# VectorE's order in the down product: the four additions to X ahead of the split of the moving operand

## The reference

```python
x = x + jnp.concatenate([ret, att], axis=-1) @ w_o[i]          # mixing, done before this stage
h = rmsnorm(x, ffn_norm_g[i])
x = x + (jax.nn.silu(h @ w_ffn_gate[i]) * (h @ w_ffn_up[i])) @ w_ffn_down[i]
gate = jax.nn.sigmoid(rmsnorm(x, ple_norm_g[i]) @ w_ple_gate[i])
x = x + gate * (p[i] @ w_ple_proj[i])
return rmsnorm(x, final_norm_g)
```

## Time and profile before

| what | value |
|---|---|
| time, median of 3 runs | 1270.57 us (1270.55 to 1271.13) |
| profiled execution, its own time | 1272.39 us |
| its span, first to last instruction | 1270.6 us |
| mean granted TensorE clock | 0.995 of full |
| TensorE (PE) busy | 1241.5 us, 98% |
| VectorE (DVE) busy | 732.4 us, 58% |
| ScalarE (ACT) busy | 480.2 us, 38% |
| GpSimd (POOL) busy | 492.5 us, 39% |

### The profile page before, as it was taken

How to read it: one execution, slowest core, us unless ns; L and a number is a source line. 1 busy time by engine, 2 the same in 40 slices (tenths; PEclk the granted TensorE clock), 3 DMA queues, 4 the chain that set the end, 5 groups by cost and what they waited for, 6 DMA issues and landing times.

```text
span 1270.6 us, 16751 instructions
## 1 busy us (share of the span) xinstructions
PE 1241.5 (98%) x6008; PEld 1043.8 (82%) x6008; DVE 732.4 (58%) x1194; ACT 480.2 (38%) x875; POOL 492.5 (39%) x510
## 2 busy tenths in 40 slices
PE   9899999989999999999999999999999999999997
PEld 8788888878888888888888888888888878788886
DVE  4554444477665326865444545444489999964433
ACT  6522222246665214533333333333354343414422
POOL 2343334441000002464334554434399887610011
PEclk9899999999999999999999999999999999999999
DMA  9411111010021500223323423323554554330002
GB/s 343 139 50 34 50 34 34 1 42 1 0 66 68 149 1 1 73 89 121 118 77 97 125 87 121 117 80 94 182 181 162 171 182 166 116 116 1 1 34 100
DMA packets 101933, 115.10 MB, mean 91 GB/s; under 512 B 4833, under 2 KB 67681, under 8 KB 101857
## 3 DMA queue, kind: packets, MB, share of 16 engines
q1 hardware_dynamic: 101424, 113.57, 27.5%
q10 hardware_dynamic: 432, 0.54, 0.1%
HBM read 90.49 MB, written 23.59 MB: 90 GB/s over the span
## 4 chain that ended last, share of the span: by engine, by line
PE 74%; issue 11%; POOL 6%; DVE 5%; DMA 2%; ACT 1%; SPq 0%; POOLq 0%; DVEq 0%; ACTq 0%
PE PS L1671 11%; PE PS L1672 10%; PE PS L1670 10%; PE PS L2004 4%; PE PS L2005 4%; PE PS L2006 4%; PE PS L206 3%; PE PS L208 3%; PE PS L207 3%; PE PS L997 3%; PE PS L1013 3%; PE PS L2356 2%; PE PS L2358 2%; PE PS L2357 2%; PE PS L791 2%
## 5 line engine op out<-in xcount | busy, mean ns | idle before, releaser
L206 PE MATMUL PS<-WF,HTH 128*128 128x512 f32 (+1 forms) x448 | 177.8, 397 | 6.8 <-DVE X L488 4.2
L208 PE MATMUL PS<-WF,HTL 128*128 128x512 f32 (+1 forms) x448 | 174.3, 389 | 0.0
L207 PE MATMUL PS<-WF,HTH 128*128 128x512 f32 (+1 forms) x448 | 174.1, 389 | 0.0
L1391 DVE TENSOR_TENSOR X<-X,PS 128x512 f32<-128x512 f32 x172 | 109.8, 677 | 51.6 <-PE PS L208 36.5
L1670 PE MATMUL PS<-HTH,WF 128*128 128x512 f32 x336 | 130.7, 389 | 0.0
L1671 PE MATMUL PS<-HTL,WF 128*128 128x512 f32 x336 | 130.7, 389 | 0.0
L1672 PE MATMUL PS<-HTH,WF 128*128 128x512 f32 x336 | 130.7, 389 | 0.0
L1603 DVE TENSOR_TENSOR WF<-RAW,WF 128x512 fp32r<-128x512 f32 x63 | 69.9, 1111 | 77.6 <-ACT WF L1593 77.6
L206 PEld LDWEIGHTS PS<-WF,HTH 128*128 128x128 f32 x448 | 85.0, 190 | 23.5 <-issue 4.9
L208 PEld LDWEIGHTS PS<-WF,HTL 128*128 128x128 f32 x448 | 84.8, 189 | 16.4
L1670 PE MATMUL PS<-WF 128*128 128x512 f32 x252 | 98.0, 389 | 0.0
(11 more groups left out here) (254 smaller groups left out, 2855.2 us busy)
## 6 DMA issues: line engine op xcount, KB each, us to landing
hid<-TMP SPq DMA_DIRECT2D x74, 256.0 KB, 2.3
TMP<-hid SPq DMA_DIRECT2D x25, 512.0 KB, 4.7
RAW<-in_w_ffn_gate SPq DMA_DIRECT2D x22, 512.0 KB, 4.1
RAW<-in_w_ffn_up SPq DMA_DIRECT2D x22, 512.0 KB, 5.4
RAW<-in_w_ffn_down SPq DMA_DIRECT2D x22, 512.0 KB, 4.1
X<-in_x SPq DMA_DIRECT2D x16, 512.0 KB, 6.0
RAW<-in_w_in SPq DMA_DIRECT2D x32, 256.0 KB, 3.6
TAB<-hid SPq DMA_DIRECT2D x9, 512.0 KB, 4.7
```

What stands on the lines that cost most here:

```text
L206: nc.tensor.matmul(dst, HTH[:, k, tok], w_h, start=(k == 0), stop=False)
L207: nc.tensor.matmul(dst, HTH[:, k, tok], w_l, start=False, stop=False)
L208: last = nc.tensor.matmul(dst, HTL[:, k, tok], w_h, start=False, stop=(k == K - 1))
L1391: nc.vector.tensor_tensor(x, x, src, ALU.add).then_inc(done, 1)
```

## The change

In the loop over the steps, the four additions come first, and the split (`ring_lo` or `down_lo`) behind them. The pieces and the two extra `down_lo` of step 33 keep their places behind both.

```diff
@@ -2087,12 +2087,12 @@
             for s in range(STEPS):
                 add_step(e, s, 0)
                 add_step(e, s, 1)
+                add_step(e, s, 2)
+                add_step(e, s, 3)
                 if s + 3 < STEPS:
                     ring_lo(e, s + 3)
                 elif s < STEPS - 1:
                     down_lo(e, LAST_ORDER[s + 3 - STEPS])
-                add_step(e, s, 2)
-                add_step(e, s, 3)
                 if s >= 18 and s % 4 == 2 and s <= 30:
                     piece_lo(e, (s - 10) // 4)
                 if s == STEPS - 2:
```

## The result

The changed kernel takes 1277.35 us (median of 6 runs, 1276.11 to 1278.16); beside it the kernel before took 1270.74 (6 runs). The ratio is 1.0050 with a 95% interval of 1.0038 to 1.0063: 6.6 us slower, forecast 4.2. The profiled execution took 1276.11 us, its span is 1274.3.

The account below looks back on a forecast made before the run. The prediction took TensorE to bound the stage, with VectorE close behind and its additions causing the stalls. Terms -0.4 + 1.6 + 0.8 + 2.2 = +4.2 us on 1270.57 gave 1274.8 us, range 1270.8 to 1277.4.

Parts of the forecast that it names:

- the tight additions: Additions of steps with s % 7 = 6, 1 or 5, needed by the next step; others have a whole step more.
- the places of the stalls: TensorE's two stalls, 1.57 and 1.62 us, stand where gate-weight pieces behind steps 18 and 26 precede tight steps 19 and 27.
- steps 0 to 17: Later splits delay GpSimd, but a margin of 1.0 us remains at the tight steps; cost 0.
- steps 18 to 23: Stall falls from 1.57 to 1.3 us, its second stall goes, steps 21 and 23 lose 0.3 more; sum -0.4 us.
- the stall before step 28: Split and both pieces of step 26 delay addition 0 of step 27; stall 3.8 us, +1.6, bounds 0 and +2.3 more.
- the end: Three splits in a row after step 33 delay step 34's additions and the next product's first matmul; +0.8 us.
- the clock: The 3.8 us stall halves TensorE's granted clock afterwards; +2.2 us, bounds 0 and 2.8.
- The split of u = 28: Split issued after addition 3 of step 25; ends at 1076.1 instead of 1074.19, with GpSimd starting at 1076.3.
- (a): The stall before step 28 grows but the clock stays: +2.0 us, 1272.6; chance 0.2.
- (b): The pair of pieces at step 26 meets no ready GpSimd operation, stall unchanged: -0.4 + 0.8, 1271.0 us; chance 0.12.
- (c): Both pieces at steps 18 and 26 pass back to back, all stalls go: -4.7 + 0.8, 1266.7 us; chance 0.05.
- (d): No margin at tight steps 1, 8, 15; missed GpSimd boundaries cost 1.4 each, two give +7.0, 1277.6 us; chance 0.08.

Follow-up runs that it names:

- e6: Changed kernel plus 14 unused matmuls on TensorE filling the stall before step 28; 1275.31 us, ratio 1.0029 to the kernel before.
- e1: New order in steps 0 to 17 alone, the kernel before's order from step 18 on; 1272.89 us, ratio 1.0010 to the kernel before.
- e2: Changed kernel, but steps 32 and 33 keep the old order; 1276.87 us, ratio 1.0034 to the kernel before.
- e4: Changed kernel with the gate-weight pieces behind steps 17, 22, 27 and 30; 1274.66 us, ratio 1.0022 to the kernel before.
- e5: Kernel before with the new order in steps 25, 26 and 27 alone; 1274.86 us, ratio 1.0026 to the kernel before.
- e10: Changed kernel run again for a second trace, nothing altered; 1276.5 us, ratio 1.0038 to the kernel before.
- e11: Kernel before run again for a second trace, nothing altered; 1271.25 us, ratio 0.9996 to the kernel before.
- e8: Changed kernel with pieces behind steps 17, 22, 24, 30 and the third gate block prepared earlier; 1268.76 us, ratio 0.9982 to the kernel before.
- e7: Kernel before with pieces behind steps 17, 22, 24, 30 and the third gate block prepared earlier; 1266.76 us, ratio 0.9960 to the kernel before.
- e9: Changed kernel with the last chunk's second GpSimd weight difference cut to 8 of 1024 columns; 1273.48 us, ratio 1.0013 to the kernel before.

## Why the prediction was right, and where its size was off

What bounds the stage, the tight additions and the places of the stalls were right. Term by term, in the stage, with the traces of the changed kernel (two) against those of before:

| term | forecast | measured |
|---|---|---|
| steps 0 to 17 | 0 | 0 (no gap in either kernel) |
| steps 18 to 23 | -0.4 | -0.2 |
| the stall before step 28 | +1.6 | +1.9 |
| the end | +0.8 | +0.8 |
| the clock | +2.2 | +1.5 and +2.5 |
| sum | +4.2 | +4.0 and +5.0 |

The stages themselves differ by 199.24 - 195.19 = 4.05 and 200.32 - 195.09 = 5.2. The steps of the working can be laid beside the trace. Addition 0 of step 8 was worked out for 977.3; it came at 976.85 in a stage that began 0.41 earlier. Addition 0 of step 19: 1039.4, came at 1039.10. The split of u = 28 was to end at 1076.1 and GpSimd to start at 1076.3; 1076.15 and 1076.33. Addition 0 of step 27: 1087.7 to 1088.1, came at 1087.66, and with the stage's earlier begin that is the later end of the two. The term of the stall that was mis-sized is "I take 3.8": it is 4.08, because the lag was carried along in full. Of steps 18 to 23, step 20 lost 0.7 less, as worked out; steps 21 and 23 lost 0.5 more, not 0.3.

The clock term was right in kind. It has two sizes, 3.4 and 6.8 us at half clock, and 2.2 lay between them. The two pieces of working in it that e6 tests, that the stall brings the fall and that the fall costs beside the stall, hold.

Rival (a), that the clock stays, is refuted by six traces in which a stall of 2.67 us or more (e1, e2, e4, e5, e10 and the changed kernel) is followed by half clock. Rivals (b) and (c) are refuted by the 5.64 us of the pair; (d) by the gapless steps 0 to 17.

Why 6.6 and not 4.1 to 5.2? The measured 1277.35 lies just inside the upper end of the stated range, 1277.4, and it is nearer to the 1277.6 of rival (d), whose reason is refuted; that the median fell inside the range is in part luck. Inside the stage the change costs 4.1 or 5.2, by the length of the fall. The rest, 1.4 to 2.5 us, lies in no stall of these traces. In the second comparison the changed kernel is 4.3 us above before, or 5.3 above e11, and its interval (3.0 to 6.5 us) and that of the first (4.8 to 8.0) overlap. The stage began anywhere from 928.4 to 932.7 in the traces shown here, all with the same work ahead of it, and that is more than the rest. The kernel before has medians from 1270.74, in the first comparison, to 1272.17, in the last; the changed kernel has 1277.35 and 1276.50, and its mean granted clock was lower in the first six runs (median 0.9925) than in the five of e10 (0.994). So both medians of the first comparison lie at the side that makes the difference large. That this is the rest is likely, but no run isolates it: it stays open how much of the 6.6 is the change's.

Where my reasons failed is e4, not the forecast: I took "tight" as a property of the next step alone. e4 and e8 show that it is one of the whole queue until VectorE has caught up.

## What to carry to other kernels

On an in-order engine that serves deadlines (here the additions that free PSUM banks), don't put two long items together, least of all ones that must take turns with another engine; put them where that other engine rests, and follow the lag until it is gone, not just to the next deadline. Where a stall of some microseconds on TensorE can't be avoided, look at the granted clock behind it: it may be paid a second time. Before reordering, read from the trace whether an instruction's long duration is its own work or its wait; with two of the pairs at 1.40 us instead of 4.82 and 4.50, and off the tight steps, the stage of e7 is 4.8 us shorter, which is more than the order of the additions cost.

## What the runs showed of the hardware

A VectorE subtraction with both inputs in SBUF waits for the end of the GpSimd operation in progress, and the wait is part of its shown duration: 1.21 us alone, up to 3.42 beside it; the additions with one input from PSUM keep 0.67 to 0.69 throughout. Of two instructions that wait for each other's engine the one that was issued first goes first, and an instruction that misses GpSimd's start by under 0.1 us (944.90 against 944.82) waits 2.3 us for it. In e9 the piece issued at 1083.22 went ahead of the GpSimd operation issued at 1083.33; in the earlier trace rows the GpSimd operation of 1036.35 went ahead of the second piece. The Trainium skill (SBUF — State Buffer, section SBUF: two separate sides) describes the ports that VectorE and GpSimd share as an exclusive lock, held for a whole instruction by whoever starts first; the durations here agree.

A stall of 2.67 us (e1) brought the clock down, one of 2.00 (e9) did not. The fall lasted 3.4 us in four traces and 6.8 in two, and 3.4 as well as 6.8 behind one and the same stall (the changed kernel and e10); what decided between them isn't shown. The fall doesn't wait for the stall's end: a matmul could have started at 1083.50 in e10 and at 1084.40 in the changed kernel, and the half clock began 2.6 and 3.9 us after that, at 1086.1 and 1088.27.
